# A mixture of experts: expert tiles taken in pairs with up products of 512 columns, and tokens gathered slot by slot

## The reference

```python
def moe_swiglu(h, router_w, wg, wu, wd):
    ...
    logits = (t @ router_w).astype(jnp.float32)
    top_logits, top_idx = lax.top_k(logits, TOP_K)
    top_w = jax.nn.softmax(top_logits, axis=-1)
    gates = jnp.einsum('tk,tke->te', top_w, jax.nn.one_hot(top_idx, N_EXPERTS, dtype=jnp.float32)).astype(h.dtype)
    y = jnp.zeros_like(t)
    for e in range(N_EXPERTS):
        y = y + gates[:, e:e + 1] * swiglu(t, wg[e], wu[e], wd[e])
    return y.reshape(bsz, s, d)
```

## Time and profile before

| | |
|---|---|
| median of 3 runs | 3039.16 us (3039.12 to 3039.36) |
| span of the profiled execution | 3033.3 us, mean granted TensorE clock 0.989 of full |
| TensorE busy over the span | 2914.4 us (96%) |
| VectorE, ScalarE, GpSimd busy | 2286.5, 1621.2, 129.2 us |
| moved | 652.11 MB, mean 215 GB/s |
| the mixture's first weight split, last down product | 2437.1 us, 3019.8 us |

### The profile page before, as it was taken

One profiled execution on the slowest core, in us unless ns is written; L12 is line 12 of the kernel. 1 busy time (PEld: TensorE's weight loads), 2 busy tenths in 40 slices (PEclk: granted clock), 3 DMA queues, 4 the chain that ended last, 5 costly groups with the idle time before them and its releaser, 6 DMA issues. The chain is left out here.

```text
span 3033.3 us, 46240 instructions
## 1 busy us (share of the span) xinstructions
PE 2914.4 (96%) x18467; PEld 2479.0 (82%) x18467; DVE 2286.5 (75%) x3619; ACT 1621.2 (53%) x2633; POOL 129.2 (4%) x151
## 2 busy tenths in 40 slices
PE   8999999999999999989999899999999799999998
PEld 7898997778888887857878688777878689999997
DVE  6456599768888887487765777767665788888888
ACT  4454433444444445374444644654345488878876
POOL 0000150000000000200000000000000200000000
PEclk9999999999999999999999999999999899999999
DMA  7344547867777775314544254324553088999895
GB/s 306 146 174 177 222 163 314 302 220 258 280 264 276 283 263 211 142 42 153 194 158 162 84 194 167 139 91 157 189 187 139 2 339 325 334 336 333 324 341 208
DMA packets 81554, 652.11 MB, mean 215 GB/s; under 512 B 6200, under 2 KB 35384, under 8 KB 38992
## 3 DMA queue, kind: packets, MB, share of 16 engines
q1 hardware_dynamic: 50160, 620.05, 54.9%
q10 hardware_dynamic: 31200, 29.36, 3.0%
HBM read 633.66 MB, written 15.73 MB: 214 GB/s over the span
## 5 line engine op out<-in xcount | busy, mean ns | idle before, releaser
L1372 PE MATMUL ps<-x_both,up_hi 128*128 128x512 f32 x1568 | 560.5, 397 | 7.2 <-DVE x_both L795 2.9
L373 DVE TENSOR_TENSOR weight_lo<-ring,weight_hi 128x1024 fp32r<-128x1024 f32 x236 | 288.2, 1230 | 207.1 <-ACT weight_hi L366 206.3
L1376 PE MATMUL ps<-x_both,up_lo 128*128 128x256 f32 x1568 | 441.4, 282 | 0.0
L1372 PEld LDWEIGHTS ps<-x_both,up_hi 128*128 128x128 f32 x1568 | 295.1, 188 | 82.2 <-DVE up_lo L1474 9.3
L366 ACT ACTIVATE weight_hi<-ring 128x1024 fp32r<-128x1024 f32 x236 | 247.9, 1059 | 127.2 <-PE ps L555 57.2
L529 PE MATMUL ps<-x_both,weight_hi 128*128 128x256 f32 x1024 | 292.7, 286 | 9.6 <-DVE x_both L795 3.3
L1376 PEld LDWEIGHTS ps<-x_both,up_lo 128*128 128x128 f32 x1568 | 296.5, 189 | 6.3
L3954 DVE TENSOR_TENSOR up_lo<-ring,up_hi 128x1024 fp32r<-128x1024 f32 x242 | 294.0, 1216 | 0.0
L530 PE MATMUL ps<-x_both,weight_hi 128*128 128x256 f32 x1024 | 289.0, 282 | 0.0
L531 PE MATMUL ps<-x_both,weight_lo 128*128 128x256 f32 x1024 | 288.8, 282 | 0.0
L3864 PE MATMUL ps<-up_hi,taken_hi 128*128 128x256 f32 x968 | 284.9, 294 | 1.8 <-DVE hidden_lo L4057 1.8
(11 more groups left out here) (663 smaller groups left out, 6345.1 us busy)
## 6 DMA issues: line engine op xcount, KB each, us to landing
ring<-in_stream SPq DMA_DIRECT2D x180, 2048.0 KB, 7.8
ring<-in_experts SPq DMA_DIRECT2D x121, 1536.0 KB, 8.5
ring<-in_stream SPq DMA_DIRECT2D x22, 1536.0 KB, 6.4
gates<-kept_gates ACTq DMA_DIRECT2D x14, 1024.0 KB, 8.9
kept_gates<-away_first ACTq DMA_DIRECT2D x8, 896.0 KB, 6.0
kept_gates<-away_last ACTq DMA_DIRECT2D x8, 896.0 KB, 7.6
params_mix<-in_mix SPq DMA_DIRECT2D x1, 3072.0 KB, 22.9
ring<-in_stream SPq DMA_DIRECT2D x4, 512.0 KB, 7.7
```

The source lines that it names most:

```text
L373: dve.tensor_tensor(self.place(self.lo, b), self.raw(b), self.place(self.hi, b), ALU.subtract).then_inc(self.split, 1)
L1372: last = pe.matmul(out, hi[:, o:o + P], x_both[:, k, :, :].rearrange("p a n -> p (a n)"), start=(n == 0), stop=(n == DK - 1), skip_group_c ...
L1376: last = pe.matmul(out[:, 0:TOKENS], lo[:, o:o + P], x_hi[:, k, :], start=False, stop=(n == DK - 1), skip_group_check=True)
```

## The change

- Tiles are taken in units: in each slot tile 0 alone, then five pairs, 6 units a slot, 66 in all. The loops of TensorE, VectorE and ScalarE run over units u.
- An up product takes both tiles of a pair: 512 moving columns (four pieces of 128 in memory), a whole bank of PSUM. A pair's up half is 12 products of 512 columns, a single tile's 12 of 256. Silu, scaling, hidden_hi and hidden_lo are one instruction a unit (128 x 256 for a pair); there are two transposes in a row for a pair, then the downs of both tiles.
- The buffers of up parts hold one unit (two tiles) in two halves of the contraction: half h of unit u is split when TensorE has used half h of unit u-1. The down parts have three places instead of two.
- Tokens are gathered slot by slot, four products of 128 columns a step, 8 steps for each slot; two steps in each of a slot's units 1 to 4. One copy of 128 x 256 keeps a step.
- Each tile's load is two transfers, up part and down part, with places and semaphores of their own; the up part waits for the up part five tiles ago to be split, the down part for the down part five tiles ago.
- Order of VectorE in unit u: hidden_lo(u), the slot's output if due, the down parts of the unit's second tile and of the next unit's first, first up half of u+2, the slot's gate if due, scale_hidden(u+1), second up half of u+2. Ahead of the loop the up parts of unit 1 come behind the first seat copy (ScalarE) and the first scaling (VectorE).

The diff, cut to its core and moved to the left:

```diff
-taken_hi = sbuf("taken_hi", [P, 3, DK, P], F32R, mem=own)
-taken_lo = sbuf("taken_lo", [P, 3, DK, P], F32R, mem=own)
-up_hi = sbuf("up_hi", [P, 2, 2, DK, P], F32R, mem=own)
-up_lo = sbuf("up_lo", [P, 2, 2, DK, P], F32R, mem=own)
-down_hi = sbuf("down_hi", [P, 2, D], F32R, mem=own)
-down_lo = sbuf("down_lo", [P, 2, D], F32R, mem=own)
+taken = sbuf("taken", [P, 2, DK, 2, P], F32R, mem=own)
+up_hi = sbuf("up_hi", [P, 2, 2, 2, DK // 2, P], F32R, mem=own)
+up_lo = sbuf("up_lo", [P, 2, 2, 2, DK // 2, P], F32R, mem=own)
+down_hi = sbuf("down_hi", [P, 3, D], F32R, mem=own)
+down_lo = sbuf("down_lo", [P, 3, D], F32R, mem=own)
...
-act_out = hT[:, 0, :].rearrange("p (a n) -> p a n", a=2)
-hid = hT[:, 1, :].rearrange("p (a n) -> p a n", a=2)
+act_out = hT[:, 0:2, :].rearrange("p b (a n) -> p b a n", a=2)
+hid = hT[:, 2:4, :].rearrange("p b (a n) -> p b a n", a=2)
...
-def chunk(g):
-    return flat[:, g % 5 * 3 * D:g % 5 * 3 * D + 3 * D]
+PER_SLOT = 6
+units = [[s * EXPERT_TILES + j for j in own_tiles] for s in range(SLOTS)
+         for own_tiles in ([0], *([j, j + 1] for j in range(1, EXPERT_TILES, 2)))]
+def up_chunk(g):
+    return flat[:, g % 5 * 2 * D:g % 5 * 2 * D + 2 * D]
+def down_chunk(g):
+    return flat[:, 10 * D + g % 5 * D:10 * D + g % 5 * D + D]
...
+def gather_bank(s, k):
+    return ps[:, 1 + k % 3 if s == 0 else 1, 0:2 * P].rearrange("p (a n) -> p a n", a=2)
+def gathers_due(u):
+    s, j = u // PER_SLOT, u % PER_SLOT
+    return [(s + 1, k) for k in (2 * j - 2, 2 * j - 1)] if s + 1 < SLOTS and 1 <= j <= DK // 2 else []
+def seat_due(u):
+    s, j = u // PER_SLOT, u % PER_SLOT
+    return s + 1 if j == PER_SLOT - 1 and s + 1 < SLOTS else None
+def downs_due(u):
+    return [g for g in (*units[u][1:], units[u][-1] + 1) if g < tiles]
...
 def _(sp):
     def load(g, src):
-        sp.dma_start(chunk(g), src).then_inc(chunk_loaded[g % 5], 16)
+        if g >= 5:
+            sp.wait_ge(up_split, up_split_of(g - 5))
+        sp.dma_start(up_chunk(g), src[:, 0:2 * D]).then_inc(up_loaded[g % 5], 16)
+        if g >= 5:
+            sp.wait_ge(down_split, g - 4)
+        sp.dma_start(down_chunk(g), src[:, 2 * D:]).then_inc(down_loaded[g % 5], 16)
...
+    def gather(s, k):
         for a, nat in enumerate((nat_hi, nat_lo)):
             for t in range(TT):
-                last = pe.matmul(gather_bank(pair, k)[:, a, :], nat[:, t, k * P:k * P + P],
-                                 seat[:, t, slots[0]:slots[-1] + 1, :].rearrange("p s n -> p (s n)"),
+                last = pe.matmul(gather_bank(s, k)[:, a, :], nat[:, t, k * P:k * P + P], seat[:, t, s, :],
                                  start=(t == 0), stop=(t == 1), skip_group_check=True)
         last.then_inc(gathered, 1)
...
+    def up(u, half):
+        s, n = u // PER_SLOT, len(units[u])
+        pe.wait_ge(up_split, up_parts_before(u, half) + n)
+        if half == 0 and u > 0 and u % PER_SLOT == 0:
+            pe.wait_ge(gather_kept, DK * (s + 1))
+        to = up_bank[:, 0:n].rearrange("p b a n -> p (b a) n")
         for k in range(4 * half, 4 * half + 4):
-            hi, lo = (buf[:, g % 2, :, k, :] for buf in (up_hi, up_lo))
-            to = up_bank.rearrange("p (a n) -> p a n", a=2)
-            if g == 0:
+            hi, lo = (buf[:, half, 0:n, :, k % 4, :].rearrange("p b a n -> p (b a) n") for buf in (up_hi, up_lo))
...
+            x_hi, x_lo = (taken[:, s % 2, k, part, :] for part in range(2))
+            pe.matmul(to, x_hi, hi, start=(k == 0), stop=False, skip_group_check=True)
+            pe.matmul(to, x_hi, lo, start=False, stop=False, skip_group_check=True)
+            last = pe.matmul(to, x_lo, hi, start=False, stop=(k == DK - 1), skip_group_check=True)
         last.then_inc(up_half, 1)
...
+    def turn_hidden(u):
+        pe.wait_ge(hid_ready, u + 1)
+        for b in range(len(units[u])):
+            last = pe.transpose(turned_bank[:, b, :], hid[:, u % 2, b, :], ident[:])
+        last.then_inc(turned, 1)
+    def down(g, b):
...
-    for g in range(tiles):
-        s, j = g // EXPERT_TILES, g % EXPERT_TILES
-        due, seat_of = gather_due(g), seat_due(g)
-        if g + 1 < tiles:
-            up(g + 1, 0)
-        pe.wait_ge(hidden_ready, g + 1)
+    for u, own_tiles in enumerate(units):
+        s, j = u // PER_SLOT, u % PER_SLOT
+        due, seat_of = gathers_due(u), seat_due(u)
+        if u + 1 < len(units):
+            up(u + 1, 0)
+        pe.wait_ge(hidden_ready, u + 1)
         if due:
-            if due[1] == 0:
-                pe.wait_ge(placed_ready, due[0] + 1)
-            gather(*due)
+            if due[0][1] == 0:
+                pe.wait_ge(placed_ready, due[0][0] // 2 + 1)
+            gather(*due[0])
         if seat_of:
             turn_seat(seat_of)
-        if g + 1 < tiles:
-            up(g + 1, 1)
+        if u + 1 < len(units):
+            up(u + 1, 1)
         if j == 0 and s > 0:
             scatter(s - 1)
-        down(g)
         if due:
-            pe.wait_ge(gather_kept, due[0] * DK + due[1] + 1)
+            pe.wait_ge(gather_kept, due[0][0] * DK + due[0][1] + 1)
+            gather(*due[1])
+        for b, g in enumerate(own_tiles):
+            down(g, b)
+        if due:
+            pe.wait_ge(gather_kept, due[1][0] * DK + due[1][1] + 1)
         if seat_of:
             pe.wait_ge(slot_gate_ready, seat_of + 1)
-        if g + 1 < tiles:
-            turn_hidden(g + 1)
+        if u + 1 < len(units):
+            turn_hidden(u + 1)
...
-    def up_low(g, half):
-        dve.wait_ge(up_high, 2 * g + half + 1)
-        dve.tensor_tensor(up_part(up_lo, g, half), raw_up(g, half), up_part(up_hi, g, half), ALU.subtract).then_inc(up_split, 1)
+    def up_low(u, half):
+        for b, g in enumerate(units[u]):
+            dve.wait_ge(up_high, up_parts_before(u, half) + b + 1)
+            dve.tensor_tensor(up_lo[:, half, b], raw_up(g, half), up_hi[:, half, b], ALU.subtract).then_inc(up_split, 1)
...
+        dve.tensor_tensor(down_lo[:, g % 3, :], down_chunk(g), down_hi[:, g % 3, :], ALU.subtract).then_inc(down_split, 1)
...
-    up_low(1, 0)
+        dve.wait_ge(acted, u + 1)
+        dve.scalar_tensor_tensor(hid[:, u % 2, 0:n, :], act_out[:, u % 2, 0:n, :], slot_gate[:, s % 2:s % 2 + 1],
+                                 up_bank[:, 0:n, 1, :], ALU.mult, ALU.mult).then_inc(hid_ready, 1)
     slot_gates(0)
     scale_hidden(0)
+    up_low(1, 0)
     down_low(0)
     up_low(1, 1)
-    up_low(2, 0)
...
+    for u, own_tiles in enumerate(units):
+        s, j, n = u // PER_SLOT, u % PER_SLOT, len(own_tiles)
+        dve.wait_ge(hidden_high, u + 1)
+        dve.tensor_tensor(hidden_lo[:, 0:n, :], turned_bank[:, 0:n, :], hidden_hi[:, 0:n, :],
+                          ALU.subtract).then_inc(hidden_ready, 1)
         if j == 0 and s > 0:
             slot_y_low(s - 1)
-        if g + 2 < tiles:
-            up_low(g + 2, 1)
-        if g + 1 < tiles:
-            down_low(g + 1)
-        if seat_due(g):
+        for g in downs_due(u):
+            down_low(g)
+        if u + 2 < len(units):
+            up_low(u + 2, 0)
+        if seat_due(u):
             slot_gates(s + 1)
-        if g + 1 < tiles:
-            scale_hidden(g + 1)
-        if g + 3 < tiles:
-            up_low(g + 3, 0)
-        if g in later_seats:
-            seats(later_seats[g]).then_inc(placed_ready, 1)
+        if u + 1 < len(units):
+            scale_hidden(u + 1)
+        if u + 2 < len(units):
+            up_low(u + 2, 1)
+        if u in later_seats:
+            seats(later_seats[u]).then_inc(placed_ready, 1)
...
+    def up_high_of(u, half):
+        if u > 0:
+            act.wait_ge(up_half, 2 * (u - 1) + half + 1)
+        for b, g in enumerate(units[u]):
+            if half == 0:
+                act.wait_ge(up_loaded[g % 5], 16 * (g // 5 + 1))
+            act.activation(up_hi[:, half, b], raw_up(g, half), ACT.Copy).then_inc(up_high, 1)
...
     def down_high_of(g):
-        act.activation(down_hi[:, g % 2, :], chunk(g)[:, 2 * D:], ACT.Copy).then_inc(down_high, 1)
...
+        act.wait_ge(down_loaded[g % 5], 16 * (g // 5 + 1))
+        if g >= 3:
+            act.wait_ge(down_done, g - 2)
+        act.activation(down_hi[:, g % 3, :], down_chunk(g), ACT.Copy).then_inc(down_high, 1)
+    def keep_gathered(s, k):
+        act.wait_ge(gathered, s * DK + k + 1)
+        act.activation(taken[:, s % 2, k], gather_bank(s, k), ACT.Copy).then_inc(gather_kept, 1)
...
-    down_high_of(0)
-    up_high_of(1, 0)
     silu(0)
     keep_seat(0)
+    up_high_of(1, 0)
+    down_high_of(0)
     up_high_of(1, 1)
-    up_high_of(2, 0)
-    up_high_of(2, 1)
-    for g in range(tiles):
...
+    for u, own_tiles in enumerate(units):
+        s, j, n = u // PER_SLOT, u % PER_SLOT, len(own_tiles)
+        due, seat_of = gathers_due(u), seat_due(u)
+        act.wait_ge(turned, u + 1)
+        act.activation(hidden_hi[:, 0:n, :], turned_bank[:, 0:n, :], ACT.Copy).then_inc(hidden_high, 1)
         if j == 0 and s > 0:
```

(21 more changed lines are left out.)

## The result

The changed kernel takes 3047.7 us (median of 6 runs, 3046.7 to 3052.51), the kernel before beside it 3039.14 us (6 runs, 3035.45 to 3042.04). The ratio is 1.0038, 95% interval 1.0028 to 1.0048: slower, by 8.6 us. The prediction had 3053, slower.

A forecast was written before the change was run, and what follows sets the result against it. The prediction took TensorE, 100% busy in the mixture, as the bound, time being the sum of its pitches. Ten slots +13.0, start +1.6 and end -0.6 gave +14 us on 3039.16, so 3053 us; range 3041 to 3066.

The forecast's parts named there:

- Gathers slot by slot: TensorE's gather steps in the first ten slots: 0.444 us each, 35.5 us where 18.7 were paid, a loss of 16.8.
- The stand at the slot's end: Last unit of each slot: TensorE stands 0.7 us for VectorE's scaling, turn at T+6.99 (T: the unit's first transpose).
- Width: Up products of 512 columns at a pitch of 0.2312 us save 1.03 us a slot, 11.4 us in all.
- The start: Start of the mixture: TensorE stands 2.6 us, then 0.8, where it stood 1.8; +1.6 us.
- The end: End of the mixture: 0.4 us of standing behind the first down, last slot saves 1.03 us; -0.6 us.
- Transfers: Each tile's load as two transfers costs nothing, hidden by 2.9 us in hand.
- From the span to the median: The median of 3039.16 us lies 5.9 us above the profiled span of 3033.3, by what is outside it; left unchanged.
- No change: Rival: stand at the slot's end absent and wide products at 0.227 us, +2, 3041 us; chance 0.16 with its neighbours.
- Faster: Rival: wide products lose nearly all their fixed part, pitch 0.215 us, 21 us less, 3032 us; chance 0.07.
- Late transfers: Rival: in ten slots, three units' closest up parts land 0.5 us late each, 15 us more, 3068 us; chance 0.14.
- a width that isn't paid for: Rival: a wide up product, its moving operand in four pieces, costs like two products, 0.240 us; 3064 us; chance 0.07.

The follow-up runs named there:

- e4_before_slotwise: The kernel before with only its gathers made slot by slot, four products of 128 columns a step; 3054.11 us, ratio 1.0065 to the kernel before.
- after: The changed kernel itself, with the whole change, against the kernel before; 3047.7 us, ratio 1.0038.
- e9_order: The changed kernel with two of VectorE's parts moved from a slot's last unit into the next slot's first unit, behind hidden_lo; 3044.95 us, ratio 1.0029.
- e5_narrow: The changed kernel with each up product of 512 columns made as two of 256; 3066.05 us, ratio 1.0098 to the kernel before.
- e2_late: The changed kernel; in a slot's last unit the next slot's first down part is split behind the silu (ScalarE) and scaling (VectorE); 3049.2 us, ratio 1.0046.
- e6_start: The changed kernel with unit 1's first up half split ahead of tile 0's silu, seat copy, gate and scaling; 3048.78 us, ratio 1.0044.
- e8_warm: The changed kernel with 18 more warm-up products in TensorE's stands at the start of the mixture; 3047.53 us, ratio 1.0038 to the kernel before.
- e1_pairs: The changed kernel with gathers for two slots at once again, two places of down parts, each unit splitting its own down parts; 3033.94 us, ratio 0.9992.
- e3_pairs_early: e1_pairs with VectorE's scaling, in a slot's last unit, ahead of the second of two up parts; 3034.8 us, ratio 0.9995 to the kernel before.
- e10_ahead: e1_pairs with the first down part of a slot's last unit split at the end of the unit before; 3024.67 us, ratio 0.9963 to the kernel before.
- e11_ahead_start: e10_ahead with the start order of e6_start; 3023.91 us, ratio 0.9964 to the kernel before.

## Why the prediction came out right, and where it did not

The sign and the size held: +14 us predicted, +8.6 by the medians, 3047.7 us inside 3041 to 3066. Part of that is luck: in the traces nine slots cost 7.4 us more where 10 were predicted, and the start with slot 0 cost 9.5 where 4.8 were, so two errors lean against each other. Step by step:

**Gathers slot by slot**: right. 0.444 us a step was taken from the eleventh slot's rows; e4_before_slotwise measures 0.44 in all slots, after has slots that are all alike. This is the term that decides the sign.

**The stand at the slot's end**: right in place, cause and size. T+6.99 was worked out, 7.01 is measured; e9_order, which leaves TensorE no wait in the loop, has a last unit of 6.27 (predicted without a stand: 6.31) and prices the stand at 0.78 us a slot with the 0.04 that the next unit loses by it.

**Width**: the mechanism was right, the term mis-sized, 1.03 us a slot predicted and 1.31 measured. Of the row of the down product, 0.231, I took the pitch; the wide product has 0.227 to 0.23. In full units (9.61 - 9.35) / 24 = 0.011 us are won with each wide product; I had 0.0086. The pitches of the products of 512 columns beside them went down as well: a scatter product follows the last by 0.227 in after, and by 0.231 in e5_narrow and 0.232 before. So the price came from neighbours that are dearer than the product it was to stand for. Full units were predicted at 9.42 and first units at 8.88, and are 9.35 and 8.79: nine slots cost 7.4 us more, not 10.

**The start**: mis-sized, by the clock. The stand of 2.6 us was there, with 2.37. But of the start's +9.5 us in the profiled pair the prediction had 4.8 (3.2 for slot 0's gathers, width and stand, 1.6 for the start). The first transpose comes 12.98 us behind the first gather instead of 9.42, which was set at no change because "the turn waits for the gate's chain as before"; the granted clock was 0.50 for most of it. Then 2.6 us go to the products at 0.43 us each, and the second stand of 0.8 disappears behind them: 4.8 + 3.6 + 2.6 - 0.8 = 10.2, near the 9.5 measured.

Do the runs without a profile pay this too? For each kernel the median less before's, beside what the traces say of the three stretches (each less before's 60.29, 471.59 and 61.65 us), and what is left of the median for the start:

| | median | start | slots 1 to 9 | end | left for the start |
|---|---|---|---|---|---|
| after | +8.6 | +9.5 | +7.4 | -0.6 | 1.7 |
| e2_late | +13.5 | +9.4 | +4.6 | -0.2 | 9.1 |
| e5_narrow | +30.4 | +10.5 | +19.2 | +0.6 | 10.5 |
| e9_order | +8.9 | +8.6 | +0.4 | -0.6 | 9.1 |
| e4_before_slotwise | +18.4 | +6.8 | +12.9 | 0.0 | 5.5 |
| e6_start | +11.7 | +4.9 | +7.4 | -0.5 | 4.8 |
| e8_warm | +10.4 | +8.1 | +7.4 | -0.5 | 3.6 |
| e1_pairs | -3.2 | +3.4 | -4.0 | +2.5 | -1.6 |
| e3_pairs_early | -2.3 | +1.7 | -3.3 | +1.5 | -0.5 |
| e10_ahead | -11.4 | +3.3 | -11.1 | -0.6 | 0.3 |
| e11_ahead_start | -12.2 | +1.5 | -11.1 | -0.6 | -0.4 |

A median's difference is uncertain by 3 to 5 us. Within that the three stretches account for most of them; e8_warm (4.5 us off) and e1_pairs (5.0) lie at the edge or just past it, and after's own is off by 8. e2_late, e5_narrow and e9_order, whose start is written as in after, pay 9 to 10.5 us for it in their medians too. So the start's cost is real there, and after's median difference is some 8 us smaller than its pieces add up to; its forecast came closer to the median than its own term for the start deserved.

Two things on record narrow this, though no run settles it. Beside the experiments the kernel before had medians 2 to 3.5 us lower than beside after. And a run's time goes with its mean granted clock, over the whole program: the kernel before took 3032.3 to 3035.3 us in its 10 runs at 0.990 or 0.991 and 3037.4 to 3041.7 in its 7 at 0.987; after took 3052.51 in its one run at 0.986, the profiled one, and 3046.7 to 3047.5 in three at 0.988. At 0.988 both have runs, and there after is 9.6 us slower (3047.1 against 3037.5 on the mean). So the 17.4 us of the profiled pair, 0.989 against 0.986, are in good part what the clock did in these two executions.

**The end**: -0.6 predicted, -0.6 measured. **Transfers**: hidden, as costed; no wait for `in_experts` is in the trace, and the loads land after 7.0 and 5.2 us. **From the span to the median**: wrong. I added the 5.9 us between the span of the profile and the median as time "outside the span". It is 1.8; the rest was that the profiled run was 4 us quicker than the median. For the difference between two medians this did no harm, but with an execution some 4 us above the median, as after's, it would have misled.

**Rivals.** No change (0.227 and no stand): its pitch was right, and the stand, whose absence it needed too, was there; in e9_order, where it is absent, the slots do come out level with before's, as the rival said. Faster (pitch 0.216): not seen, the wide products have 0.227 to 0.23. The Trainium skill, TensorE: Matmul & The Clock Gate, section Back-to-back issue gap, gives 131 ns a product at 512 columns in a sustained stream of weight loads and products. No row here agrees with it: the wide products have 0.227 in the median, the warm-up's 0.215. Late transfers and a width that isn't paid for are excluded for after by the waits and by e5_narrow; with shorter slots (e1_pairs) loads do come late.

**Open.** Why after's own comparison shows so little of the start. Why the clock falls at 2441.8 in after and not in before: e8_warm filled the gaps that lay ahead, and it was low all the same. How much e6_start, e8_warm and e11_ahead_start win at the start (1.4 to 4.6 us in their traces): by the table it may be in their medians, but the runs of the kernel before alone spread from 3032 to 3042 us. And whether one load a tile would serve the changed kernel as well wasn't tried.

## To carry to other kernels

Where an engine is full, count the operations that a change adds by the price of their pitch, not by their size: a product of 128 columns costs 93% of one of 256 here, so work done for two slots at once is nearly free for the second. If an engine that is off the critical path is late at one place, moving its work behind that place moves the stand to the next unit (e2_late, e3_pairs_early); work that goes ahead, or far enough back to a unit with time in hand, ends it (e10_ahead, e9_order). And take a span's distance to the median from several runs, since the profiled one may lie off the median by more than the change is worth.

## What the runs showed of the hardware

- The pitch of a product of 512 columns depends on its neighbours: down and scatter products are 0.231 to 0.232 us apart before, mostly 0.227 among wide up products. What sets it is open.
- Four products of 128 columns cost 0.44 us where four of 256 cost 0.476, and make the product that follows start its successor late (0.17 us instead of 0.12 in e4_before_slotwise, 0.28 instead of 0.23 in after).
- At the lower clock level a wide product has a pitch of 0.43 us (0.23 at the higher). The level fell behind stretches in which TensorE was busy for 2.41 and for 0.99 of 3.40 us, and in e8_warm it stayed low from 2431.3 to 2448.4 while TensorE was busy throughout. Why is open.
- The time of a run goes with its mean granted clock: the kernel before took 3036.4 us on the mean in 13 runs at 0.989, 3038.6 in 7 at 0.987.
- At 322 to 332 GB/s over a slot (after) no engine waited for a load; in e1_pairs, whose short slots move 341 to 350 GB/s, ScalarE waited 14.2 us for loads.
